# Two mixing layers of a fused float32 model: input columns by pairs of heads, head steps between quarters of the projections, roots of norms on GpSimd

## The chip, the cores and the metric

One program on one core of a Trainium2 chip, one launch. The metric is the device time of the launch in microseconds (us), the median over runs. All data is float32, and the program streams 533.57 MB through the core.

## The reference, cut to what matters

The model is an embedding norm, two layers (a hybrid mixer, then a dense FFN in layer 0 and a mixture of experts in layer 1), then a second block (FFN, gating with dilated attention, cross attention, FFN). The change is in the two hybrid mixers, and in small operations of the dilated attention.

```python
def hybrid_mixer(x, w_in, q_norm_g, kv_norm_g, w_uq, w_ukv, beta_mla, beta_moba, w_o, ...):
    h = x @ w_in                                  # (256, 1024) @ (1024, 2656)
    c_q, c_kv, k_rope, rq, rk, rv, rg, mq, mk, mv = jnp.split(h, splits, axis=-1)
    o_a = rms_norm(mla_attention(c_q, c_kv, k_rope, ...), beta_mla)   # 6 heads, softmax
    o_b = retention(rq, rk, rv, rg, cos_b, sin_b)                     # 5 heads, no softmax, gated
    o_c = rms_norm(moba_attention(mq, mk, mv), beta_moba)             # 5 heads, softmax
    return jnp.concatenate([o_a, o_b, o_c], axis=-1) @ w_o            # (256, 1024) @ (1024, 1024)
```

The MLA heads take queries and keys of 96 columns from two small products (`w_uq`, `w_ukv`) of the normed latents `c_q`, `c_kv`. The other heads have 64 columns. Sequence length is 256: with 128 partitions, every matrix has two row tiles, t = 0 and 1.

## The kernel before, in words

Every weight matrix is cut into chunks of at most 128 x 2048 and streamed by SyncE into a ring of six `raw` buffers. A product in float32 is made of three products in a faster format: ScalarE copies a chunk into `whi` (the high part, L837), VectorE subtracts it and leaves the rest in `wlo` (the low part, L1158), and TensorE runs `mm3` (L350 to L352): whi x high, wlo x high, whi x low part of the activations. `whi` and `wlo` have three slots each (`SPLIT`). The calls `advance(n)` in the streams of ScalarE and VectorE fix where these splits stand in the in-order queue of each engine. The order of all work is written out by hand, engine by engine, with semaphores: `ev0`/`ev1` count evacuated row tiles, `s`, `sf`, `mx`, `p`, `tp`, `pt`, `od`, `o` count the stages of heads, `sd` the square roots, `xh`/`xt` the high and low parts of turned activations.

One mixer runs in four stages, one after the other:

1. `project` (PE): `x @ w_in` in five groups of 512 columns (two chunks each: a group has 4 quarters of 12 matmuls, by half of the depth and row tile) and a last group of 96. ScalarE (L880) and VectorE (L1239) evacuate to `h`. Squares, square roots (L1026, L1027 on ScalarE), scaling and turning of the latents lie beside it, and so does one rotation of all ten retention queries and keys at 128 x 320.
2. The two latent products, `ukv` and `uq`.
3. `heads`: 16 heads, 5 retention, 5 MoBA, 6 MLA, as a software pipeline over steps. A head is turned (q and k, four transposes, L615), copied to `qkt` (ScalarE, L977), scored (L632, L633; retention L629, L630), masked (VectorE, L1417), its maximum taken (L1429, L1430), exponentiated (ScalarE, L981, L983), turned again (L641), copied (L1425), multiplied with v (L659 to L661) and divided (L1443). Everything has two PSUM banks. The retention norm (`retention_sums`, L1374 to L1382, and `retention_norm`, L1390, L1394), and the norms of MoBA and MLA with their square roots on ScalarE (L989, L996, L1048) are placed in it or after it.
4. All of `r` is turned (`transpose_x`, L366), split, and multiplied with `w_o` (two groups of 512 columns, in PSUM banks 4 to 7).

The dilated attention of the second block uses the same `heads` code with 8 heads.

## Time and profile before

| | |
|---|---|
| median of 3 runs | 2351.25 us (2330.93 to 2351.82) |
| span of the profiled execution | 2349.9 us, 1.35 us less than the median |
| mean granted TensorE clock | 0.929 |
| instructions | 27258 |

No time of its own is recorded for the profiled execution besides its span; what lies around it is taken as the 1.35 us between the span and the median. In the rows below, a line of a timeline is: start, duration, engine, source line, operation, output <- inputs, shapes, count, and in brackets the idle time before it with what ended it. A matmul's duration includes its pipeline; the pace of matmuls is read from the distance of their starts. PEclk is the granted clock as a share of full speed: 1.00 is 2.4 GHz, 0.50 is 1.2 GHz.

### The profile page before, as it was taken

To read this page: it belongs to the slowest core of one execution; us is meant where nothing else is said; L and a number is where in the kernel's file an instruction comes from. 1 tells how busy PE (TensorE), PEld (TensorE's weight loads), DVE (VectorE), ACT (ScalarE), POOL (GpSimd) and SP (SyncE) were. 2 spreads that over 40 slices of the span, in tenths; PEclk is the share of its full clock that TensorE was granted. 3 is DMA by queue.
4 is the path that set the end of the run, shared out by engine and by line. 5 is a ranking of instruction groups with operands and counts; after the bars stand their busy time and mean duration, and the time that the engine had idled before them with its cause. 6 is when DMAs were issued, how large, how long until landed. Compare 5 with 4: busy or idle time off the path is not lost.

```text
span 2349.9 us, 27258 instructions
## 1 busy us (share of the span) xinstructions
PE 2177.7 (93%) x9892; PEld 1789.4 (76%) x9892; DVE 1539.9 (66%) x1558; ACT 1260.3 (54%) x1323; POOL 10.8 (0%) x24
## 2 busy tenths in 40 slices
PE   6978998998699999989999999999799888988997
PEld 5856886876578887878787888878588776877886
DVE  5555545644678888878887888888645564544443
ACT  4343343433367677767776677777443445434433
POOL 0000000000000000000000000000000000000000
PEclk9869999956799999999999999999899995999999
DMA  7304554411289999979997998999455350433550
GB/s 296 144 1 152 188 188 146 155 54 54 101 315 362 352 352 352 352 302 348 353 362 307 345 362 341 362 351 373 164 184 191 128 212 1 179 126 118 194 182 35
DMA packets 74407, 533.57 MB, mean 227 GB/s; under 512 B 8432, under 2 KB 8432, under 8 KB 10448
## 3 DMA queue, kind: packets, MB, share of 16 engines
q1 hardware_dynamic: 72000, 519.77, 58.6%
q0 software_dynamic: 2320, 12.56, 1.5%
q8 instruction: 65, 1.06, 0.2%
q14 instruction: 22, 0.18, 0.0%
HBM read 531.25 MB, written 1.05 MB: 227 GB/s over the span
## 4 chain that ended last, share of the span: by engine, by line
PE 89%; DVE 6%; ACT 3%; issue 1%; DMA 1%; POOL 0%; DVEq 0%; ACTq 0%; SPq 0%; POOLq 0%
PE ps L350 26%; PE ps L352 26%; PE ps L351 26%; PE ps L486 1%; PE ps L537 1%; PE ps L515 1%; PE ps L366 1%; PE ps L633 1%; PE ps L615 1%; PE ps L659 1%; PE ps L632 1%; PE ps L458 1%; ACT whi L837 1%; PE ps L641 1%; PE ps L661 1%
## 5 line engine op out<-in xcount | busy, mean ns | idle before, releaser
L1158 DVE TENSOR_TENSOR wlo<-raw,whi 128x2048 fp32r<-128x2048 f32 x500 | 1135.4, 2274 | 440.6 <-ACT whi L837 436.4
L837 ACT ACTIVATE whi<-raw 128x2048 fp32r<-128x2048 f32 x500 | 949.7, 1901 | 342.6 <-PE ps L352 332.2
L350 PE MATMUL ps<-whi,xth 128*128 128x512 f32 (+1 forms) x1872 | 749.3, 400 | 25.4 <-DVE wlo L1158 10.1
L352 PE MATMUL ps<-whi,xtl 128*128 128x512 f32 (+1 forms) x1872 | 731.8, 391 | 0.0
L351 PE MATMUL ps<-wlo,xth 128*128 128x512 f32 (+1 forms) x1872 | 731.0, 390 | 0.0
L350 PEld LDWEIGHTS ps<-whi,xth 128*128 128x128 f32 x1872 | 358.3, 191 | 100.7 <-issue 20.2
L352 PEld LDWEIGHTS ps<-whi,xtl 128*128 128x128 f32 x1872 | 357.8, 191 | 75.4
L351 PEld LDWEIGHTS ps<-wlo,xth 128*128 128x128 f32 x1872 | 359.0, 192 | 70.2 <-issue 1.7
L350 PE MATMUL ps<-whi,hth 128*128 128x512 f32 (+2 forms) x736 | 287.5, 391 | 6.6 <-DVE htl L1260 4.5
L352 PE MATMUL ps<-whi,htl 128*128 128x512 f32 (+2 forms) x736 | 286.6, 389 | 0.0
L351 PE MATMUL ps<-wlo,hth 128*128 128x512 f32 (+2 forms) x736 | 286.0, 389 | 0.0
L350 PEld LDWEIGHTS ps<-whi,hth 128*128 128x128 f32 x736 | 139.2, 189 | 35.0 <-issue 5.4
L352 PEld LDWEIGHTS ps<-whi,htl 128*128 128x128 f32 x736 | 139.1, 189 | 27.9
L351 PEld LDWEIGHTS ps<-wlo,hth 128*128 128x128 f32 x736 | 139.2, 189 | 27.3
L928 ACT ACTIVATE prob<-ps 128x256 f32<-128x256 f32 x112 | 43.0, 384 | 91.7 <-PE ps L352 91.7
L893 ACT ACTIVATE prob<-ps 128x256 f32<-128x256 f32 x66 | 21.7, 381 | 126.0 <-PE ps L352 126.0
L934 ACT ACTIVATE hth<-ps 128x256 fp32r<-128x256 f32 x112 | 43.1, 384 | 82.7 <-PE ps L515 82.7
L897 ACT ACTIVATE hth<-ps 128x512 fp32r<-128x512 f32 x33 | 19.8, 599 | 104.3 <-PE ps L458 104.3
L1255 DVE TENSOR_TENSOR probt<-prob,ps 128x256 f32<-128x256 f32 x66 | 24.9, 418 | 66.6 <-ACT prob L893 66.6
L1417 DVE SCALAR_TENSOR_TENSOR prob<-ps,cst 128x384 f32<-128x384 f32 x30 | 16.7, 557 | 67.8 <-PE ps L633 67.8
L1260 DVE TENSOR_TENSOR htl<-ps,hth 128x512 fp32r<-128x512 f32 x33 | 22.8, 691 | 55.3 <-ACT hth L897 55.3
L366 PE MATMUL ps<-cst,r 128*128 128x128 f32 x112 | 23.8, 400 | 34.3 <-DVE r L1234 22.1
(276 smaller groups left out, 1510.5 us busy)
## 6 DMA issues: line engine op xcount, KB each, us to landing
raw<-in_stream SPq DMA_DIRECT2D x493, 1024.0 KB, 4.8
bc<-in_rows POOLq DMA_DIRECT2D x5, 1024.0 KB, 5.1
cst<-in_consts POOLq DMA_DIRECT2D x1, 2180.0 KB, 12.6
raw<-in_stream SPq DMA_DIRECT2D x4, 384.0 KB, 3.1
raw<-in_stream SPq DMA_DIRECT2D x2, 576.0 KB, 3.6
r<-in_x POOLq DMA_DIRECT2D x2, 512.0 KB, 4.6
bc<-in_rows POOLq DMA_DIRECT2D x2, 512.0 KB, 4.4
bc<-in_mem POOLq DMA_DIRECT2D x1, 1024.0 KB, 5.1
```

The source lines that it names most:

```text
L350: pe.matmul(o, ah, bh, start=start, stop=False, skip_group_check=True)
L351: pe.matmul(o, ah, bl, start=False, stop=False, skip_group_check=True)
L352: return pe.matmul(o, al, bh, start=False, stop=stop, skip_group_check=True)
L366: m = pe.transpose(ps[banks[k // 2]][:, (k % 2) * S + t * P:(k % 2) * S + (t + 1) * P], src[:, t, k * P:(k + 1) * P], ident)
L458: m = pe.transpose(ps[2][:, k * S + t * P:k * S + (t + 1) * P], hs[:, t, k * P:(k + 1) * P], ident)
L486: m = pe.matmul(ps[bank][:, k * P:(k + 1) * P], x[:, t, (4 * g + k) * P:(4 * g + k + 1) * P], onehot[:, e, t, :], start=(t == 0), stop=(t ...
L515: m = pe.transpose(ps[1][:, k * P:(k + 1) * P], hs[:, 0, k * P:(k + 1) * P], ident)
L837: act.activation(whi[:, c.split, 0:c.width], raw[:, c.raw, 0:c.width], ACT.Copy).then_inc(hi_done, 1)
L928: act.activation(sg[:, 0, :], ps[0][:, 0:FU], ACT.Silu).then_inc(sem("e_sg"), 1)
L934: act.activation(hth[:, 0:2, 0:P], ps[1][:, 0:2 * P].rearrange("p (k s) -> p k s", k=2), ACT.Copy).then_inc(sem("e_hh"), 1)
L1158: dve.tensor_tensor(wlo[:, c.split, 0:c.width], raw[:, c.raw, 0:c.width], f32(whi[:, c.split, 0:c.width]), ALU.subtract).then_inc(lo_done, 1)
L1255: m = dve.tensor_tensor(hs[:, t, :], sg[:, t, :], ps[t][:, FU:2 * FU], ALU.mult)
```

## The change

- **Layout and widths.** The input columns are reordered on the host: latents and one gate (480), then five groups with q, k, v of a *pair* of heads and the gate of one retention head (448, 448, 448, 448, 384). All six groups come in two chunks (12 in place of 11), and the latent weights come after the fourth chunk. Each row tile of a group has a PSUM bank of 4 to 6.
- **Pairs.** q and k of a pair are turned together (four transposes for two heads); the second head of a pair is scored from partitions 64 to 127 of `qkt`. The order of heads is retention 0, 1, MLA 0 to 5, retention 2, 3, 4, MoBA 0 to 4 (`WORK`).
- **Placement.** Step i of the pipeline does turn(i), outputs(i-3) or, for retention, outputs(i-2), turn_p(i-2), scores(i-1). Steps 0 to 13 stand behind quarters of groups 2 to 5, steps 14 and 15 behind the last quarter, 16 to 18 between quarters of the first half (by depth) of the output product. The turning of `r` and the output product are in two halves: depth 0 to 511 (MLA and two retention heads) first. The stages of a head have one PSUM bank each (scores bank 0, turned probabilities bank 1, turned q and k bank 7), only the outputs have two.
- **Masks.** Mask and maximum are one `tensor_tensor_reduce` per row tile (`masked`), the division is one `tensor_tensor` for both (`normed`); this holds for the dilated heads too.
- **Roots.** Reciprocal square roots of the latent, retention, MLA and MoBA norms are computed by GpSimd (`inverse_root`: multiply-add, then power -0.5). The retention gate uses Tanh in place of Silu, with one more VectorE operation (`retention_gates`).
- **Rotation** of retention queries and keys is done by pairs, for both row tiles in one operation (`rotate_pair`), at the start and in steps 2 and 6.

```diff
+PAIRS = ((("ret", 0), ("ret", 1)), (("ret", 2), ("ret", 3)), (("ret", 4), ("moba", 0)),
+         (("moba", 1), ("moba", 2)), (("moba", 3), ("moba", 4)))
+PAIR_OF = {head: (p, s) for p, pair in enumerate(PAIRS) for s, head in enumerate(pair)}
+
+
+WORK = (list(PAIRS[0]) + [("mla", n) for n in range(MLA_H)] + list(PAIRS[1]) + list(PAIRS[2]) + list(PAIRS[3])
+        + list(PAIRS[4]))
...
+IN_GROUPS = 6
+IN_WIDTHS = [C_PAIR, W_PAIR, W_PAIR, W_PAIR, W_PAIR, W_PAIR - HD]
+STEPS_BY_GROUP = {2: {3: [0], 4: [1]}, 3: {1: [2], 2: [3], 3: [4], 4: [5]}, 4: {1: [6], 2: [7], 3: [8], 4: [9]},
+                  5: {1: [10], 2: [11], 3: [12], 4: [13]}}
+ROTATE_AT = {2: 1, 6: 2}
+GATES_AT, MLA_SQUARES_AT, RET_SUMS_AT, SCALE_AT = 10, 12, 13, 14
+B_TQ, B_S, B_TP, B_O = 7, 0, 1, 2
...
+    _in = [KD // 2 * _w for _w in IN_WIDTHS for _ in range(2)]
+    STREAM += [(f"in{_l}", _in[0:4]), (f"uq{_l}", [2 * 576]), (f"ukv{_l}", [768]), (f"inb{_l}", _in[4:]),
+               (f"o{_l}", PROJ * 2)]
...
+            def inverse_root(ready, dst, means, eps_value):
+
+                pool.wait_ge(*ready)
+                for a, b, src, scale in means:
+                    m = pool.tensor_scalar(var[:, a:b], src, scale, eps_value, ALU.mult, ALU.add)
+                link(m)
+                pool.tensor_tensor(dst, var[:, means[0][0]:means[-1][1]], half[:, 0:means[-1][1] - means[0][0]],
+                                   ALU.pow).then_inc(sem("rs"), 1)
...
                 rows(2 + 4 * l, 2, ("emb" if l == 0 else "ln2_0", "x"), T)
+                inverse_root(at(f"lat{l}", "sq", 1), rstd[:, :], ((0, 2, ss[:, 0:2], 1.0 / 256), (2, 4, ss[:, 2:4], 1.0 / 128)), RMS_EPS)
+
+                inverse_root((sem(f"ret{l}_var"), 1), gs[:, 3, 0:10], ((4, 14, gs[:, 1, 0:10], 4.0 / HD),), 4.0 * RMS_EPS)
+                inverse_root(at(f"mla{l}", "sq", 1), rstd[:, 0:2], ((0, 2, ss[:, 0:2], 1.0 / 384),), RMS_EPS)
+                inverse_root(at(f"moba{l}", "sq", 1), rstd[:, 2:4], ((2, 4, ss[:, 2:4], 1.0 / 320),), RMS_EPS)
...
+                def step(i):
+
+                    if i < len(WORK):
                         turn_qk(i)
-                    if 0 <= i - 3 < len(work) and not soft[i - 3]:
+                    if 0 <= i - 3 < len(WORK) and SOFT[i - 3]:
                         outputs(i - 3)
-                    if i >= 4 and soft[i - 4]:
-                        outputs(i - 4)
-                    if 3 <= i < len(work) + 3:
-                        turn_p(i - 3)
-                    if 1 <= i < len(work) + 1:
+                    if 0 <= i - 2 < len(WORK) and not SOFT[i - 2]:
+                        outputs(i - 2)
+                    if 0 <= i - 2 < len(WORK) and SOFT[i - 2]:
+                        turn_p(i - 2)
+                    if 0 <= i - 1 < len(WORK):
                         scores(i - 1)
...
+                for j, t in ((0, 0), (0, 1), (1, 0), (1, 1)):
+                    in_part(0, j, t)
+                for j, t in ((0, 0), (0, 1), (1, 0)):
+                    in_part(1, j, t)
+                transpose_x(f"lat{l}", h, kn=3, banks=(0, 1))
+                in_part(1, 1, 1)
+                pe.wait_ge(*at(f"lat{l}", "xt", 1))
+                latent(f"uq{l}", 288, (0, 2), lambda t, part: UQ_BANKS[2 * t + part], free_uq)
+                pe.wait_ge(*at(f"lat{l}", "xt", 2))
+                latent(f"ukv{l}", 384, (2, 3), lambda t, part: 2 * t + part, lambda t, part: None)
+                for g in range(2, IN_GROUPS):
+                    for n, (j, t) in enumerate(((0, 0), (0, 1), (1, 0), (1, 1))):
+                        in_part(g, j, t)
+                        for i in STEPS_BY_GROUP[g].get(n + 1, ()):
+                            step(i)
+                step(14)
+                step(15)
+                turn_mix(0, (5, 7))
+                o_part(0, 0, 0)
+                step(16)
+                o_part(0, 0, 1)
+                step(17)
+                o_part(0, 1, 0, range(0, 2))
+                step(18)
+                o_part(0, 1, 0, range(2, 4))
+                o_part(0, 1, 1)
+                turn_mix(1, (0, 1))
+                for n in range(2):
+                    for t in range(T):
+                        o_part(1, n, t)
 
             pe.wait_ge(sem("ident_in"), 16)
...
+            def softmax(stage, n, count):
+
+                act.wait_ge(*at(stage, "mx", count))
+                act.activation(prob[:, n % 2, 0:P], prob[:, n % 2, 0:P], ACT.Exp, bias=nmax[:, n, 0:1], scale=-1.0,
+                               accum_out=rsum[:, n, 0:1])
+                act.activation(prob[:, n % 2, P:3 * P], prob[:, n % 2, P:3 * P], ACT.Exp, bias=nmax[:, n, 1:2], scale=-1.0,
+                               accum_out=rsum[:, n, 1:2]).then_inc(sem("p"), 1)
...
+                def step(i):
+
+                    g = 2 + i // 4
+                    if g < IN_GROUPS and i % 4 < 2:
+                        evac_in(g, i % 4)
+                    if i < len(WORK) and (i == 0 or UNIT_OF[i - 1] != UNIT_OF[i]):
+                        u = UNIT_OF[i]
+                        d = QD if UNITS[u][0] == "mla" else P
+                        act.wait_ge(*at(hd, "tq", u + 1))
+                        act.activation(qkt[0:d, u % 2, :], ps[B_TQ][0:d, :], ACT.Copy).then_inc(sem("qk"), 1)
+                    if i % 2 == 0:
+                        advance(in_chunk(l, 7 + i // 2) if i <= 8 else AT[f"o{l}"] + min((i - 10) // 2, 2))
+                    if 0 <= i - 1 < len(WORK) and SOFT[i - 1]:
+                        softmax(hd, i - 1, soft_before(i))
+                    if i == GATES_AT:
...
+                    if i == MLA_SQUARES_AT:
+                        act.wait_ge(*at(hd, "o", WORK.index(("mla", MLA_H - 1)) + 1))
+                        act.wait_ge(sem(f"gated{l}"), 1)
+                        squares(f"mla{l}", [(r[:, t, 0:384], h[:, t, 0:384], ss[:, t:t + 1]) for t in range(T)])
+
...
+            def masked(n, bank, mask, scale):
+
+
+                for t, a, b in ((0, 0, P), (1, P, 3 * P)):
+                    m = dve.tensor_tensor_reduce(out=prob[:, n % 2, a:b], in0=ps[bank][:, a:b], in1=mask[:, a:b], scale=-scale,
+                                                 scalar=-NEG, op0=ALU.add, op1=ALU.min, accum_out=nmax[:, n, t:t + 1])
...
+            def normed(stage, n, bank, col, count):
+
+                dve.wait_ge(*at(stage, "od", n + 1))
+                dve.wait_ge(*at(stage, "ri", count))
+                dve.tensor_tensor(r[:, :, col:col + HD], ps[bank][:, 0:2 * HD].rearrange("p (t d) -> p t d", t=T),
+                                  rinv[:, n, :].unsqueeze(2).to_broadcast([P, T, HD]), ALU.mult).then_inc(sem("o"), 1)
...
+                def step(i):
+
+                    if 0 <= i - 3 < len(WORK) and SOFT[i - 3]:
+                        dve.reciprocal(rinv[:, i - 3, :], rsum[:, i - 3, :]).then_inc(sem("ri"), 1)
+                        take_outputs(i - 3)
+                    if 0 <= i - 2 < len(WORK) and not SOFT[i - 2]:
+                        take_outputs(i - 2)
+                    if 0 <= i - 2 < len(WORK) and SOFT[i - 2]:
+                        n = i - 2
+                        dve.wait_ge(*at(hd, "tp", soft_before(n + 1)))
+                        dve.tensor_copy(probt[:, n % 2, 0:3 * P], ps[B_TP][:, 0:3 * P]).then_inc(sem("pt"), 1)
+                    if 0 <= i - 1 < len(WORK):
+                        weigh(i - 1)
+                    if i % 2 == 0:
+                        advance(in_chunk(l, 7 + i // 2) if i <= 8 else AT[f"o{l}"] + min((i - 10) // 2, 2))
+                    if i == 17:
+                        advance(AT[f"o{l}"] + 3)
+                    if i in ROTATE_AT:
+                        rotate_pair(ROTATE_AT[i])
+                    if i == GATES_AT:
+                        retention_gates()
+                    if i == RET_SUMS_AT:
+                        retention_sums()
+                    if i == SCALE_AT:
+                        retention_norm()
+                        scale(f"mla{l}", 0, 0, 384)
+
+                advance(in_chunk(l, 3))
+                dve.wait_ge(*at(st, "ev0", 1))
...
+                    link(dve.tensor_copy(kc[:, t, :, NOPE:QD],
+                                         h[:, t, C_ROPE:C_RG].unsqueeze(1).to_broadcast([P, MLA_H, ROPE])))
+                dve.sem_inc(sem(f"kv{l}"), 1)
+                rotate_queries()
+                advance(in_chunk(l, 6))
...
+                split_mix(0, (5, 7))
+                for i in range(16, 19):
+                    step(i)
+                scale(f"moba{l}", 2, O_MOBA, D)
+                split_mix(1, (0, 1))
 ```

On TensorE, a step of the MLA heads in layer 0 (L615, L791: turn q and k; L659 to L661, L834 to L836: outputs; L641, L819: turn probabilities; L632/L633, L811/L812: scores). Before:

```order
L615 MATMUL ps<-cst,qc 96x128 [waits qk]
L615 MATMUL ps<-cst,qc 96x128
L615 MATMUL ps<-cst,kc 96x128 x2
L659 MATMUL ps<-h,probt 128x64 [waits o,pt]
L660 MATMUL ps<-h,probt 128x64
L661 MATMUL ps<-h,probt 128x64
L641 MATMUL ps<-cst,prob 128x128 [waits p]
L641 MATMUL ps<-cst,prob 128x128 x2
L632 MATMUL ps<-qkt 128x128 [waits sf,qk]
L633 MATMUL ps<-qkt 128x256
```

In the changed kernel a step, and the beginning of the quarter of twelve matmuls that follows it (L420 to L422 are `mm3`):

```order
L791 MATMUL ps<-cst,qc 96x128 [waits rope0,qk]
L791 MATMUL ps<-cst,qc 96x128
L791 MATMUL ps<-cst,kc 96x128 x2
L834 MATMUL ps<-vc,probt 128x64 [waits o,pt]
L835 MATMUL ps<-vc,probt 128x64
L836 MATMUL ps<-vc,probt 128x64
L819 MATMUL ps<-cst,prob 128x128 [waits pt,p]
L819 MATMUL ps<-cst,prob 128x128 x2
L811 MATMUL ps<-qkt 128x128 [waits mx,qk]
L812 MATMUL ps<-qkt 128x256
L420 MATMUL ps<-whi,xth 128x448 [waits lo_done]
L421 MATMUL ps<-wlo,xth 128x448
```

Before, the next step follows at once; now a quarter of the input product stands between two steps, and the scores wait for the maximum of the head before.

On VectorE, the retention norm's sums in layer 0 (L1374 to L1382, L1681 to L1689). Before, in step 10 of `heads`, with nine steps to come:

```order
L1443 TENSOR_SCALAR r<-ps,rinv 128x64
L1374 TENSOR_REDUCE gs<-r 128x10 [waits o]
L1375 TENSOR_SCALAR gs<-gs 128x10 [waits dve_chain]
L1378 TENSOR_TENSOR r<-r,gs 128x320 [waits dve_chain]
L1378 TENSOR_TENSOR r<-r,gs 128x320
L1381 TENSOR_TENSOR h<-r 128x2x320 [waits dve_chain]
L1382 TENSOR_REDUCE gs<-h 128x10 [waits dve_chain]
L1417 SCALAR_TENSOR_TENSOR prob<-ps,cst 128x384 [waits s]
```

In the changed kernel they stand in step 13; what follows them in step 14, up to the split of an output chunk (L1403) and the norm (L1707, L1710), is:

```order
L1689 TENSOR_REDUCE gs<-h 128x10 [waits dve_chain]
L1752 RECIPROCAL rinv<-rsum 128x2
L1624 TENSOR_TENSOR r<-ps,rinv 128x2x64 [waits ri,od]
L1759 COPY probt<-ps 128x384 [waits tp]
L1616 ISA prob,nmax<-ps,cst 128x128 [waits s]
L1616 ISA nmax 128x1
L1616 ISA prob,nmax<-ps,cst 128x256
L1616 ISA nmax 128x1
L1403 TENSOR_TENSOR wlo<-raw,whi 128x2048 [waits hi_done]
L1707 TENSOR_TENSOR r<-r,gs 128x320 [waits rs]
L1707 TENSOR_TENSOR r<-r,gs 128x320
L1710 TENSOR_TENSOR r<-r,h 128x2x320 [waits dve_chain]
```

The sums, a chunk's split and the norm now stand in three successive steps, with head work that TensorE waits for behind each of them.

On ScalarE, the end of the heads in layer 0: squares of MLA, square root and split of all of `r`. Before:

```order
L1046 ACTIVATE prob,ss<-r 128x384 [waits o]
L1046 ACTIVATE prob,ss<-r 128x384
L1048 ACT_TABLE_LOAD
L1048 ACTIVATE sd<-ss,eps 128x2 [waits act_chain]
L855 ACTIVATE xth<-ps,cols 128x256 [waits tr]
```

In the changed kernel, the squares of MoBA (the root is on GpSimd) and the split of the second half:

```order
L1216 ACTIVATE h,ss<-r 128x320 [waits o]
L1216 ACTIVATE h,ss<-r 128x320
L1225 ACTIVATE xth<-ps,cols 128x256 [waits tr]
L1225 ACTIVATE xth<-ps,cols 128x256
L1225 ACTIVATE xth<-ps,cols 128x256 [waits tr]
```

The table load and the root are gone from ScalarE's queue, and between the squares and the split there is now GpSimd, VectorE's scaling and TensorE's turning.

## Rows read from the trace of the kernel before

**Rows 1.** The page: busy time of the engines, and the chain by engine.

```profile
PE 2177.7 (93%) x9892; PEld 1789.4 (76%) x9892; DVE 1539.9 (66%) x1558; ACT 1260.3 (54%) x1323; POOL 10.8 (0%) x24
PE 89%; DVE 6%; ACT 3%; issue 1%; DMA 1%; POOL 0%; DVEq 0%; ACTq 0%; SPq 0%; POOLq 0%
```

**Rows 2.** Busy time by stage; columns in the first line, the first is the stretch.

```profile
core 0: us, PE busy (x) PEld busy (x) DVE busy (x) ACT busy (x) POOL busy (x), PEclk, DMA share, GB/s
23.45:195.84 172.39, 156.52 (x699) 128.50 (x699) 90.45 (x188) 67.80 (x124) 0.00 (x0) 0.81 0.32 123
86.81:92.32 5.51, 5.51 (x38) 5.27 (x37) 2.97 (x3) 4.64 (x3) 0.00 (x0) 1.00 0.34 144
92.32:171.95 79.63, 63.76 (x273) 50.68 (x274) 40.84 (x134) 31.54 (x87) 0.00 (x0) 0.62 0.07 27
409.85:587.78 177.93, 163.93 (x699) 135.44 (x699) 90.20 (x191) 70.34 (x128) 0.00 (x0) 0.75 0.25 90
479.80:565.89 86.09, 72.09 (x274) 57.38 (x274) 40.31 (x134) 31.32 (x87) 0.00 (x0) 0.52 0.06 22
1938.90:1981.40 42.50, 38.27 (x136) 27.71 (x136) 16.89 (x58) 17.32 (x48) 0.00 (x0) 0.50 0.00 1
```

**Rows 3.** TensorE's timeline: 512-column matmuls at full clock.

```profile
193.80 0.39 PE L350 MATMUL ps<-whi,xth 128*128 128x512 f32 x1
...
195.61 0.39 PE L352 MATMUL ps<-whi,xtl 128*128 128x512 f32 x1
```

**Rows 4.** TensorE's timeline: one MLA step at full clock, to the next step's start.

```profile
142.64 0.43 PE L659 MATMUL ps<-h,probt 128*128 128x64 f32 x2 [0.73 <-DVE probt L1425]
...
144.57 0.38 PE L615 MATMUL ps<-cst,kc 128*96 128x128 f32 x2
145.69 0.43 PE L659 MATMUL ps<-vc,probt 128*128 128x64 f32 x2 [0.74 <-DVE probt L1425]
```

**Rows 5.** Groups by line and form, 23.45 to 195.84: count, busy us, mean ns.

```profile
L1158 DVE TENSOR_TENSOR wlo<-raw,whi 128x2048 fp32r<-128x2048 f32 x15 | 34.3, 2291 | 32.4 <-ACT whi L837 31.1 <-issue 1.3
...
L1417 DVE SCALAR_TENSOR_TENSOR prob<-ps,cst 128x384 f32<-128x384 f32 x11 | 6.1, 557 | 19.7 <-PE ps L633 19.7
...
L1425 DVE COPY probt<-ps 128x384 f32<-128x384 f32 x11 | 5.9, 540 | 1.2 <-PE ps L641 1.2
...
L983 ACT ACTIVATE prob<-prob,nmax 128x256 f32<-128x256 f32 x11 | 5.4, 493 | 0.0
...
L1430 DVE TENSOR_REDUCE nmax<-prob 128x1 f32<-128x256 f32 x11 | 4.5, 409 | 0.0
...
L1429 DVE TENSOR_REDUCE nmax<-prob 128x1 f32<-128x128 f32 x11 | 3.0, 277 | 0.1
```

**Rows 6.** VectorE's timeline: the retention sums, first and last instruction.

```profile
134.88 0.81 DVE L1374 TENSOR_REDUCE gs<-r 128x10 f32<-128x640 f32 x1
...
137.72 0.82 DVE L1382 TENSOR_REDUCE gs<-h 128x10 f32<-128x640 f32 x1
```

**Rows 7.** Timeline from the turning of `r` to the output product, layer 0.

```profile
167.62 3.68 PE L366 MATMUL ps<-cst,r 128*128 128x128 f32 x16 [3.99 <-DVE r L1515]
170.06 2.30 ACT L855 ACTIVATE xth<-ps,cols 128x256 fp32r<-128x256 f32 x6 [3.15 <-PE ps L366]
...
171.95 0.77 PE L350 MATMUL ps<-whi,xth 128*128 128x512 f32 x1 [0.65 <-DVE xtl L1178]
```

**Rows 8.** Windows with the granted clock (columns as in rows 2).

```profile
94.80:128.00 33.20, 33.13 (x119) 26.16 (x120) 12.12 (x45) 9.82 (x23) 0.00 (x0) 0.50 0.12 49
140.00:154.00 14.00, 10.02 (x75) 8.28 (x74) 8.38 (x31) 9.08 (x28) 0.00 (x0) 1.00 0.00 0
466.00:470.00 4.00, 4.00 (x38) 4.00 (x36) 2.05 (x2) 1.41 (x2) 0.00 (x0) 0.98 0.51 203
470.00:474.00 4.00, 4.00 (x18) 4.00 (x19) 0.26 (x1) 0.87 (x1) 0.00 (x0) 0.50 0.71 258
```

**Rows 9.** GpSimd's groups, the whole run.

```profile
L336 POOL DMA_DIRECT2D kc<-in_spatial x1 | 0.9, 905 | 0.0
...
L311 POOL MEMSET eps<- 128x1 f32 x1 | 0.1, 98 | 0.3 <-POOLq L1833 0.3
```

717 lines of the change are left out of this document (422 added, 295 removed).

## The prediction, made before the changed kernel was run

> **What bounds the kernel now.** I read the page first: TensorE is busy 93% of the span and makes up 89% of the chain that ended last, far ahead of VectorE at 6% [rows 1]. So only two things shorten the run: less TensorE work, or the same work at a better pace. Next the windows by stage [rows 2]: a mixer, from the first input matmul to the last output matmul, takes 172.39 us in layer 0 and 177.93 in layer 1, together 350.3. Of these, the heads with the turning of `r` take 79.63 and 86.09. In both, TensorE is busy for only 63.76 and 72.09, and the granted clock is 0.62 and 0.52: this stage pays for waits and for the slow clock. Last the timelines, for the price of one piece.
>
> At full clock 512-column matmuls start 0.226 apart (8 steps from 193.80 to 195.61, [rows 3]). Narrow ones do not follow their columns all the way: the 96-column group issues 38 in 4.00 us, 0.105 each [rows 8]. An MLA step takes 3.05 us, of which 0.74 is waiting, so 2.31 are work [rows 4]. A MoBA step saves half of its turning with pairs (0.28), a retention step also the turning of probabilities (0.33; both estimates from the same step): 2.03 and 1.70.
>
> **TensorE's work after the change, at full clock, per mixer.** By columns from 0.226 per 512: 480, 448 and 384 columns cost 0.212, 0.199 and 0.172. The input product has 48 matmuls of each group: 48 x (0.212 + 4 x 0.199 + 0.172) = 56.6. Before it is 48 x (5 x 0.226 + 0.105) = 59.3, so 2.7 us of narrow matmuls go. Latent products 5.2 (their 36 matmuls in the 5.51 of [rows 2]), turning of latents 0.8. Heads: 6 x 2.31 + 5 x 2.03 + 5 x 1.70 = 32.5. Output product 96 x 0.226 = 21.7. Turning of `r` 1.8.
>
> **What hides what.** A quarter of a 448-column group is 12 x 0.199 = 2.4 us and now stands between two steps. Between the scores of a head and its turn_p TensorE has this quarter, a turning and the outputs of an older head: 2.4 + 0.45 + 0.7 = 3.5 us. The other engines need in that time the mask with maximum and two exponentials. The exponentials I take as 1.35 (0.493 for the wide one, [rows 5], a little less for the narrow one, two readouts). `tensor_tensor_reduce` does not occur in the trace. Below, it is bounded by the mask alone, 0.56, above by twice mask and two maxima, 2 x (0.56 + 0.41 + 0.28) = 2.5 [rows 5]. I take 1.0, nearest to the 1.25 of the three operations that it replaces. With 0.2 for semaphores the chain is 2.6, so it fits, unless a split (2.29 for a full chunk, [rows 5]) or a rotation stands ahead in VectorE's queue. Going through steps 0 to 13 by these prices, VectorE is late four times: 0.4 at the start (evacuation of k and v and rotation of queries before the split of the seventh chunk), 1.9 at step 4 (a split and a rotation of six operations stand before the first softmax head's mask), 0.2 and 0.6 later. That is 3.1 us of stall. For the latent chain, three quarters (7.2 us) hide evacuation, squares, root and scaling (about 3.8), so it costs nothing; GpSimd has 3.4 us of slack there.
>
> So from the first input matmul to the end of step 13: 56.6 + 0.8 + 5.2 + head work of steps 0 to 13, which is 32.5 less 7.3 for what stands later (five outputs, four turn_p, three scores, a turning) = 25.2, + stalls 3.1 = 90.9. The first 13 matmuls of layer 0 and the first 5 of layer 1 still run at half clock, as before: + 2.6 and + 1.0.
>
> **The tail.** Here no quarters are left, and VectorE sets the pace. From the end of step 13 on TensorE: mask of head 12 1.35 (it starts behind the split of a chunk); sums of the retention norm 3.6 (134.88 to 138.54, [rows 6]); step 14: division, copy, mask 2.05 (0.5 + 0.54 + 1.0), split 2.3, norm and scaling 2.5 (about two thirds of the sums: two instructions of 320, one of 640, two of 384 columns); step 15: 2.05. Sum 13.9. Before, these sums stood beside eight more heads. Then the exponentials of head 14 (1.35), which stand in ScalarE's queue before the split of the first half of `r`, and 1.9 from its start to the first output matmul (170.06 to 171.95, [rows 7]): 17.2. Then two quarters of 2.7 with step 16 of 1.8 between, 7.2, and 3.1 more for the part of it at half clock, since TensorE has stood idle several times before. Then high and low part of the last output chunk in a row, 1.95 + 2.3; behind it on VectorE stand the last head's division 0.5, squares 0.95, GpSimd's root 0.6, scaling 0.7; TensorE's three remaining quarters (2.7 each, and steps 17 and 18) lie beside this. Then turning and split 2.9, and the second half of the output product, 48 x 0.226 = 10.9. Together 17.2 + 10.3 + 4.3 + 2.75 + 2.9 + 10.9 = 48.4.
>
> GpSimd's two instructions are bounded by the smallest and largest of its rows, 2 x 0.1 and 2 x 0.9 [rows 9]; I take 0.6. Only the MoBA root is exposed. The retention root has 4.3 us of cover (step 14 up to the split); this cover is VectorE's own queue.
>
> The Trainium skill (GPSIMD Engine Reference, Instruction dispatch) says that the first call of a freshly loaded kernel pays about 6 us that no instruction shows. No run here shows it yet. By it the first latent root would outlast its 3.4 us of slack by about 3 us, once, and the sum would be 3 us higher.
>
> **Sum.** Layer 0: 90.9 + 2.6 + 48.4 = 141.9; layer 1: 90.9 + 1.0 + 48.4 = 140.3; together 282.2 against 350.3, a gain of 68.1. The table loads for square roots that stood on the path are in the stages that are replaced whole. The dilated heads run at 0.50 and TensorE is busy 38.27 of 42.50 [rows 2], so a shorter softmax chain gives nothing; the longer mask instruction now stands before the copy that the outputs wait for, about 0.4 late in eight steps less what is covered: + 1.5. Everything else is unchanged. 2349.9 - 68.1 + 1.5 = 2283.3, and with the 1.35 around the span 2284.7; I give 2285.
>
> **Rivals.**
> A. *Chains bind every step.* The mask instruction costs its upper bound 2.5, and copies of `qkt`, evacuations and high parts (1.9) stand before the exponentials on ScalarE. Then the 3.5 us between scores and turn_p do not suffice. Price: 1.5 more less 0.9 slack, some ten steps, 6 us; 1.5 in each of three tail steps, 4.5; one GpSimd root at its upper bound, 1.2; ScalarE's order 0.5 in ten steps, 5: 16.7 per mixer, 33 in all, 2318. For it: single PSUM banks make each step wait for the one before. Against: VectorE was busy only 90 of 172 us in a mixer and has little more to do now.
> B. *The clock stays at half in the interleaved stretch* (slower). From group 2 to the middle of the output product there are 36.8 + 10.9 of dense matmuls and 32.5 of head work. At half clock these double, + 80, less stalls and waits that it swallows (about 16): 64 per mixer, 128 in all, 2413. It decides from about half of the stretch at half clock on, where the gain of 68 is gone. For it: 33 us of head work without a gap ran at 0.50 [rows 8], and in layer 1 the clock fell at 470 in the middle of 96-column matmuls, with TensorE busy without a gap [rows 8]. Against: before those narrow ones, 512-column matmuls held 1.00, and head work with 4 us of 14 idle held 1.00 from 140 to 154. The Trainium skill (TensorE: Matmul & The Clock Gate, HAM oscillation) blames idle gaps alone; by that rule the stretch stays at full clock, but the trace does not agree at 470, so B stays open.
> C. *Better cover in the tail.* If VectorE works through sums, mask and split faster than I priced (mask at 0.56) and the clock does not fall there: 4 + 3.1 + 3.1 of stalls, 10 per mixer, 2265.
>
> **How the numbers follow.** Forecast 58%, A 23%, B 8% (a third of it only part of the stretch, near 2350), C 11%. About what can be told from no change here is 1%, 24 us. Faster by over 1% needs less than 2327.7: forecast, C and nearly all of A give 0.88; B in part and A at its worst 0.06 within 1%; B in full 0.06 slower. The range takes in C and A with its bounds: 2255 to 2330, which leaves out B.
>
> **What would show it.** Right: from group 2 on TensorE starts a quarter within about 0.1 of the end of a step, at clock 1.00; MLA steps at a period near 4.7 us; VectorE without idle from the sums to the split of `r`; TensorE idle about 11 us around steps 14 and 15 (17.2 less the 6 or so of work in it), and a clock of 0.50 after it. A mixer takes 140 to 142 us. Wrong: turn_p waiting for the exponentials in each step (A), PEclk of 0.50 in the windows of groups 3 to 5 (B), a GpSimd instruction of several us before the latents' scaling, or a `tensor_tensor_reduce` far from 0.5 us per instruction.

## The result, and the profile after

The changed kernel takes 2277.78 us (median of 4 runs, 2271.92 to 2278.76) against 2341.09 for the kernel before beside it: a ratio of 0.970, 95% interval 0.966 to 0.974. Timed again later (a_again2) it took 2266.12 (2264.79 to 2279.18), ratio 0.971 (0.967 to 0.974). The forecast was 2285 us. The kernel before spreads wider than the changed one, from 2328.49 to 2351.82 us in its four runs here, and its trace (span 2349.9) is of one of the longest, while the trace of the changed kernel (span 2270.1) is of the shortest of its four. So the gain is 63 us by the medians here, 78 by those of a_again2 and its neighbours (2344.02 before), and 79.8 between the two traces.

The page after, with the lines that answer to [rows 1]:

```profile
PE 2117.5 (93%) x9852; PEld 1752.4 (77%) x9852; DVE 1517.7 (67%) x1556; ACT 1249.0 (55%) x1313; POOL 24.2 (1%) x43
PE 90%; DVE 6%; ACT 2%; issue 1%; DMA 1%; POOL 0%; DVEq 0%; SPq 0%; ACTq 0%; POOLq 0%
```

The shares say almost nothing: TensorE was the bound and still is. What shows the change is the busy time by stage, to be read beside [rows 2]. First the whole mixer of layer 0, from the first input matmul to the end of the last output matmul, then layer 1's, then the dilated heads:

```profile
21.73:159.05 137.32, 128.70 (x679) 112.14 (x679) 82.21 (x187) 61.03 (x118) 6.60 (x9) 0.95 0.43 155
...
373.32:508.21 134.89, 126.81 (x679) 110.78 (x679) 81.66 (x190) 63.25 (x122) 6.60 (x9) 0.94 0.37 131
...
1855.44:1896.89 41.45, 36.84 (x134) 26.54 (x135) 11.99 (x58) 17.21 (x48) 0.00 (x0) 0.51 0.00 1
```

The mixers went from 172.39 + 177.93 = 350.3 us to 272.2: 78.1 of the 79.8 us by which the span fell (2349.9 to 2270.1). TensorE's busy time in them fell by 65 (320.5 to 255.5) and its idle time by 13 (29.9 to 16.7), and the granted clock rose from 0.81 and 0.75 to 0.95 and 0.94. With two levels only, twice the missing share is the time at half clock: an estimate from these rows is 154 us before and 30 after. So the larger part of the gain is the same work at the faster clock. The remaining 1.7 us is a sum of small differences of both signs, of which one is chance: TensorE waits once or twice in a run, 5 to 6 us each, for weights among the experts' chunks (once in the changed kernel, `PE ps L420 <- DVE wlo L1403: 5.8, 1, 5.8` between 700 and 1500 us; 10.9 in two for e2_two_part_mask below). What lies outside the mixers, which no edit below but those of the mask touches, takes 1987.5 (e3_roots_scalar) to 2004.2 us (e6_apart_filled) in the traces; these waits are a part of that spread. It moves whole runs by more than some edits below are worth. So I compare the mixers in the traces (from the start of the first input matmul to 0.23 us behind the start of the last output matmul) and the times beside them.

Where the half clock went is shown by windows along layers 0 and 1:

```profile
30.00:110.00 80.00, 80.00 (x467) 73.30 (x466) 50.12 (x127) 42.00 (x76) 1.42 (x3) 1.00 0.48 173
110.00:120.00 10.00, 6.71 (x41) 5.27 (x40) 9.44 (x22) 7.08 (x20) 2.23 (x3) 0.96 0.32 106
120.00:130.00 10.00, 6.65 (x20) 4.82 (x21) 6.60 (x18) 2.45 (x9) 2.07 (x2) 0.50 0.28 107
130.00:140.00 10.00, 10.00 (x48) 8.06 (x47) 2.51 (x10) 2.91 (x5) 0.00 (x0) 0.86 0.00 0
...
380.00:460.00 80.00, 80.00 (x468) 73.34 (x467) 50.09 (x127) 42.05 (x76) 1.42 (x3) 1.00 0.43 154
```

In these 80 us (quarters and latent products, and from 57.95 on steps between the quarters) TensorE has no idle time and clock 1.00. Then the quarters are used up: 6.7 of 10 us busy, VectorE 9.44 of 10, and the clock falls. TensorE's timeline of one MLA step with its quarter, to the next step:

```profile
76.89 0.38 PE L791 MATMUL ps<-cst,qc 128*96 128x128 f32 x2
...
77.94 0.50 PE L819 MATMUL ps<-cst,prob 128*128 128x128 f32 x3
...
78.50 0.60 PE L812 MATMUL ps<-qkt 96*128 96x256 f32 x2
78.75 0.56 PE L420 MATMUL ps<-whi,xth 128*128 128x448 f32 x1
...
81.38 0.38 PE L791 MATMUL ps<-cst,qc 128*96 128x128 f32 x2
```

The quarter starts at 78.75, straight behind the scores, and the next step comes 4.49 us after this one, without a bracket of idle time. Before, a step alone took 3.05 with 0.74 of waiting [rows 4], at full clock, which it had for a small part of the stage only.

VectorE's timeline in the tail, from the mask of head 12 to the scaling:

```profile
113.30 0.28 DVE L1616 CUSTOM_DVE_ANT_0 prob<-ps,cst 128x128 f32<-128x128 f32 x1
113.50 0.08 DVE L1616 DVE_READ_ACCUMULATOR2_ANT nmax<- 128x1 f32 x1
113.50 0.42 DVE L1616 CUSTOM_DVE_ANT_0 prob<-ps,cst 128x256 f32<-128x256 f32 x1
113.85 0.08 DVE L1616 DVE_READ_ACCUMULATOR2_ANT nmax<- 128x1 f32 x1
113.85 0.81 DVE L1681 TENSOR_REDUCE gs<-r 128x10 f32<-128x640 f32 x1
...
118.91 2.29 DVE L1403 TENSOR_TENSOR wlo<-raw,whi 128x2048 fp32r<-128x2048 f32 x1
121.12 0.89 DVE L1707 TENSOR_TENSOR r<-r,gs 128x320 f32<-128x320 f32 x2
...
122.78 0.74 DVE L1715 TENSOR_SCALAR r<-r,rstd 128x384 f32<-128x384 f32 x2
```

No line carries an idle bracket, and none does until the mask of head 14 ends at 125.01: up to there this queue sets the pace. Then ScalarE's exponential of head 14 and its split of `r` stand on the path:

```profile
125.05 0.40 ACT L1182 ACTIVATE prob<-prob,nmax 128x128 f32<-128x128 f32 x1 [5.03 <-DVE nmax L1616]
...
125.94 1.54 ACT L1225 ACTIVATE xth<-ps,cols 128x256 fp32r<-128x256 f32 x4
```

TensorE's three longest waits (outputs of head 12, turning of `r`, first output matmul; the last is for both engines) are:

```profile
118.50 0.43 PE L834 MATMUL ps<-h,probt 128*128 128x64 f32 x2 [2.10 <-DVE probt L1759]
...
123.25 1.97 PE L860 MATMUL ps<-cst,r 128*128 128x128 f32 x8 [0.70 <-DVE r L1715]
127.80 0.77 PE L420 MATMUL ps<-whi,xth 128*128 128x512 f32 x1 [2.58 <-DVE xtl L1723]
```

### The profile page after: what moved, and what is told of

Read it like the earlier page. It is cut to its first block, busy times and chain, and to the rows that moved or that the text cites. A ratio compares the mean times of both kernels' runs of the same rounds, so it can differ in the third digit from the quotient of the medians.

```text
span 2270.1 us, 27254 instructions
## 1 busy us (share of the span) xinstructions
PE 2117.5 (93%) x9852; PEld 1752.4 (77%) x9852; DVE 1517.7 (67%) x1556; ACT 1249.0 (55%) x1313; POOL 24.2 (1%) x43
## 4 chain that ended last, share of the span: by engine, by line
PE 90%; DVE 6%; ACT 2%; issue 1%; DMA 1%; POOL 0%; DVEq 0%; SPq 0%; ACTq 0%; POOLq 0%
PE ps L420 27%; PE ps L422 27%; PE ps L421 26%; PE ps L554 1%; PE ps L605 1%; PE ps L583 1%; DVE wlo L1403 1%; PE ps L436 1%; ACT whi L1045 1%; PE ps L526 1%; DVE r L1459 0%; DVE resid L1450 0%; PE ps L791 0%; DMA raw<-in_stream 0%; DVE xtl L1417 0%
## 5 line engine op out<-in xcount | busy, mean ns | idle before, releaser
L1403 DVE TENSOR_TENSOR wlo<-raw,whi 128x2048 fp32r<-128x2048 f32 (+4 forms) x502 | 1135.4, 2265 | 401.9 <-ACT whi L1045 397.3
L1045 ACT ACTIVATE whi<-raw 128x2048 fp32r<-128x2048 f32 (+4 forms) x502 | 950.1, 1894 | 284.2 <-PE ps L422 281.2
L420 PE MATMUL ps<-whi,xth 128*128 128x512 f32 (+3 forms) x1872 | 754.4, 403 | 26.8 <-DVE wlo L1403 10.2
L422 PE MATMUL ps<-whi,xtl 128*128 128x512 f32 (+3 forms) x1872 | 732.0, 391 | 0.0
L421 PE MATMUL ps<-wlo,xth 128*128 128x512 f32 (+3 forms) x1872 | 731.3, 391 | 0.0
L420 PEld LDWEIGHTS ps<-whi,xth 128*128 128x128 f32 x1872 | 359.2, 192 | 101.9 <-issue 21.5
L421 PEld LDWEIGHTS ps<-wlo,xth 128*128 128x128 f32 x1872 | 359.8, 192 | 67.2 <-issue 1.7
L420 PE MATMUL ps<-whi,hth 128*128 128x512 f32 (+2 forms) x736 | 286.5, 389 | 6.6 <-DVE htl L1505 4.5
L421 PE MATMUL ps<-wlo,hth 128*128 128x512 f32 (+2 forms) x736 | 285.0, 387 | 0.0
L420 PEld LDWEIGHTS ps<-whi,hth 128*128 128x128 f32 x736 | 138.5, 188 | 35.0 <-issue 5.4
L421 PEld LDWEIGHTS ps<-wlo,hth 128*128 128x128 f32 x736 | 138.5, 188 | 27.3
L1136 ACT ACTIVATE prob<-ps 128x256 f32<-128x256 f32 x112 | 43.0, 384 | 91.9 <-PE ps L422 91.9
L1105 ACT ACTIVATE hth<-ps 128x512 fp32r<-128x512 f32 x33 | 19.7, 598 | 104.4 <-PE ps L526 104.4
L436 PE MATMUL ps<-cst,resid 128*128 128x128 f32 x64 | 15.7, 427 | 38.2 <-DVE resid L1450 38.2
L1546 DVE TENSOR_TENSOR htl<-ps,hth 128x256 fp32r<-128x256 f32 x112 | 46.8, 418 | 0.0
```

The costliest lines, as they stand in the source:

```text
L420: pe.matmul(o, ah, bh, start=start, stop=False, skip_group_check=True)
L421: pe.matmul(o, ah, bl, start=False, stop=False, skip_group_check=True)
L422: return pe.matmul(o, al, bh, start=False, stop=stop, skip_group_check=True)
L436: m = pe.transpose(ps[banks[k // 2]][:, (k % 2) * S + t * P:(k % 2) * S + (t + 1) * P], src[:, t, k * P:(k + 1) * P], ident)
L1045: act.activation(whi[:, c.split, 0:c.width], raw[:, c.raw, 0:c.width], ACT.Copy).then_inc(hi_done, 1)
L1136: act.activation(sg[:, 0, :], ps[0][:, 0:FU], ACT.Silu).then_inc(sem("e_sg"), 1)
```

## The experiments

Mixer lengths are those of layers 0 and 1 in the profiled run. The changed kernel has 137.3 and 134.9 (136.0 and 134.7 in a_again2).

**a_again2: the changed kernel unchanged.**

> The changed kernel as it is, timed beside the kernels of this group: 2272 to 2280 us, mixers of 137.3 and 134.9 us in the trace.

Measured: 2266.12 us, below the range I gave, with mixers 1.3 and 0.2 us shorter than in the first trace. Differences of some 1.5 us in a mixer and of 10 us between medians therefore say nothing by themselves. Each mixer length here is from one trace.

**e1_apart: the input side of the placement undone.** The evacuations and splits of groups 2 to 5 move ahead of the steps on ScalarE and VectorE too.

```
-  in_part(g, j, t)
-  for i in STEPS_BY_GROUP[g].get(n + 1, ()):
-      step(i)
-step(14)
+  in_part(g, j, t)
+for i in range(15):
+    step(i)
```

> The changed kernel with one thing undone: steps 0 to 13 of the heads all follow the last quarter of the input product (pairs, masks in one instruction and roots on GpSimd stay). Theory (the placement carries the gain, because the steps' TensorE work of 25 us then runs at clock 1.00 and their chains lie beside the quarters): set apart, the same steps run at clock about 0.5 and wait for VectorE and ScalarE, 50 to 58 us instead of 25, so each mixer grows by 25 to 33 us, and the time is 2328 to 2345 us. Rival (the gain comes from less work: pairs of heads, masks, roots): the mixers grow by no more than 8 us each, under 2295 us.

Measured: 2310.72 us (2304.36 to 2318.82), ratio to before 0.988 (0.982 to 0.994); mixers 155.9 and 151.6. Between theory and rival: steps 0 to 13 take 43.0 us (89.80 to 132.84) and not 50 to 58. The windows show why:

```profile
89.80:114.00 24.20, 17.56 (x123) 14.51 (x121) 13.54 (x57) 11.81 (x34) 0.00 (x0) 1.00 0.00 1
114.00:134.90 20.90, 18.43 (x68) 14.77 (x69) 11.77 (x28) 8.79 (x19) 0.00 (x0) 0.52 0.23 82
```

The clock stayed at 1.00 for 24 us of steps with TensorE idle a quarter of the time, and fell afterwards. In that first part the MLA steps come 2.96 us apart (turnings at 105.11 and 108.07), against 2.31 of work: the chain through mask and exponential sets them. So the 18.6 and 16.7 us that the mixers grew come from both, chains in the open and, later, half clock.

**e2_two_part_mask: the mask in two kinds of instruction.**

```
-m = dve.tensor_tensor_reduce(out=prob[..], in0=ps[bank][..], in1=mask[..], scale=-scale,
-                             scalar=-NEG, op0=ALU.add, op1=ALU.min, accum_out=nmax[..])
+link(dve.scalar_tensor_tensor(out=prob[..], in0=ps[bank][..], scalar=-scale, in1=mask, op0=ALU.mult, op1=ALU.add))
+m = dve.tensor_reduce(nmax[..], prob[..], AX, ALU.min)      # twice
```

> The changed kernel, its masks in two kinds of instruction again (scale and mask over 384 columns, then two minima), in both mixers and in the dilated heads. A mask then takes about 1.35 us instead of the 0.63 that the changed kernel's trace shows. Theory (VectorE is on the path only in the tail): in steps 0 to 13 it is hidden; steps 14 to 16 hold two masks on the path, +1.5 us a layer, and the last two dilated heads +1 each: 5 us more in all, 2281 to 2286 us. Rival (VectorE paces every step): 11 soft heads at 0.72 us in both layers, 16 us more, 2294 us.

Measured: 2280.86 us, ratio 0.974 (0.969 to 0.978); mixers 138.8 and 138.5, together 5.1 more. The median is at the theory's size. The traces show 9.0 us: beside the 5.1, 3.9 in the dilated heads (45.34 us from 1864.79 to 1910.13, where the changed kernel has 41.45). The rival's 16 us would be in the mixers and are not. The longer mask takes 1.20 us (113.56 to 114.76), and even so TensorE waits only once, 0.19 us, between 30 and 112 us.

**e5_apart_mask: both together.** Head steps apart, and the longer mask.

> e1_apart (steps 0 to 13 behind the whole input product) and e2_two_part_mask (the mask in two kinds of instruction) in one kernel. Between the quarters the longer mask cost 5.1 us over both mixers (138.8 and 138.5 against 137.3 and 134.9). Theory (quarters cover the chains, and without them the chain of a step, scores to mask to exponential to turning, sets the pace): with the steps apart the 0.72 us of 11 soft heads come back in full and TensorE idles more, so its clock falls earlier; each mixer is 8 to 15 us longer than in e1_apart (155.9 and 151.6), time 2327 to 2341 us. Rival (the mask costs the same wherever the steps stand): 2 to 3 us a mixer, about 2316 us.

Measured: 2331.17 us, ratio 0.995 (0.992 to 0.998); mixers 164.8 and 161.9 (21.21 to 186.04 and 399.95 to 561.82), 8.9 and 10.2 more than e1_apart. The same edit costs 19.1 us with the steps apart and 5.1 beside the quarters. The theory holds, at the lower end of its range.

**e7_output_apart: the output side of the placement undone.**

```
+for i in range(16, 19):
+    step(i)
 turn_mix(0, (5, 7))
 o_part(0, 0, 0)
-step(16)
 o_part(0, 0, 1)
-step(17)
-o_part(0, 1, 0, range(0, 2))
-step(18)
-o_part(0, 1, 0, range(2, 4))
+o_part(0, 1, 0)
```

> The changed kernel with the output side of the placement undone: steps 16 to 18 stand ahead of the turning of the mixture and the output product, steps 0 to 13 stay between the input quarters. Theory (the last two heads' chains lie beside the first output quarters): mask, exponential, turning and copy of heads 14 and 15 are then waited for, the first output matmul comes 7 to 9 us later, of which the 3.6 us of work of steps 16 to 18 and the waits before the second turning come back: 2 to 5 us a mixer, 2277 to 2287 us against the 2266 to 2278 us of the changed kernel. Rival (VectorE's queue sets the time of the output product anyway, so the heads' place there does not matter): mixers within 1 us of 137.3 and 134.9.

Measured: 2280.80 us, ratio 0.971 (0.969 to 0.973); mixers 142.7 and 140.9, 5.4 and 6.0 more. The first output matmul starts at 136.00 instead of 127.80. The theory's direction holds, its price of 2 to 5 us a mixer was too low, and the rival is out. The whole time is 3 us above the changed kernel's first median and 15 above its second, so it tells nothing finer.

**e8_all_apart: both sides apart and the longer mask.**

> Both sides of the placement and the one-instruction mask undone together (e5_apart_mask and e7_output_apart in one kernel). What then is left of the change are the pairs of heads with their layout of the input columns, the roots on GpSimd, and the joint division. Theory (placement and mask are nearly the whole gain): mixers of 166 to 171 us, 2340 to 2350 us, the kernel before within 1%. Rival (pairs and the rest of the work saved are worth more than that): mixers no longer than e5_apart_mask's 163.5 and 159.8 us, 27 us below the kernel before.

Measured: 2341.83 us, ratio 0.998 (0.995 to 1.001); mixers 170.8 and 168.3. The theory holds. (The mixers of e5_apart_mask in the expectation were read too short; they are the 164.8 and 161.9 above, and the rival is out by either.) With the mixers of before (350.3) this makes a ledger of the 78.1 us, in this order: everything else (pairs with their layout, roots, joint division, rotation by pairs, the output product in halves) 11.2 (to 339.1); output side of the placement 12.4 (to 326.7); short mask 19.1 (to 307.6); input side 35.4 (to 272.2). The order matters: the mask is worth 5.1 and the output side 11.3 when taken away alone from the changed kernel. The 11.2 are the difference of two traces; the medians beside each other differ by 5.0 us, with an interval of the ratio that takes in 1, and how the 11.2 divide was not tried.

**e3_roots_scalar: square roots on ScalarE, reciprocals on VectorE.**

```
-inverse_root(at(f"mla{l}", "sq", 1), rstd[:, 0:2], ...)     # GpSimd, and three more
+act.activation(sd[:, n:n + 2], ss[:, n:n + 2], ACT.Sqrt, bias=eps[:, 1:2], scale=1.0 / width)
+link(dve.reciprocal(rstd[:, n:n + T], sd[:, n:n + T]))
```

> The changed kernel with the roots of the mixers' norms on ScalarE again (square root with its table load, then a reciprocal on VectorE). Theory (GpSimd saves table loads only where ScalarE is awaited): the retention and MLA roots hide behind VectorE's split, the latents' behind the product, and only the last root, +1.3 us of table load and +0.2 of reciprocal less 0.9 of GpSimd, shows: 1 to 3 us more in all, 2279 to 2281 us. Rival (every table load is on the path): four a layer at 1.3 us, 10 us more, 2288 us.

Measured: 2275.79 us (2266.05 to 2277.99), ratio 0.972 (0.968 to 0.976); mixers 139.1 and 137.5, 1.8 and 2.6 more. ScalarE's timeline with three of the table loads:

```profile
121.44 1.28 ACT L1255 ACT_TABLE_LOAD   x1
...
123.24 1.28 ACT L1177 ACT_TABLE_LOAD   x1
127.45 0.40 ACT L1177 ACTIVATE prob<-prob,nmax 128x128 f32<-128x128 f32 x1 [2.93 <-DVE nmax L1622]
...
146.00 1.28 ACT L1209 ACT_TABLE_LOAD   x1
```

The load at 123.24 costs nothing: it lies in a wait for VectorE that lasts to 127.45. The one at 121.44 is seen: VectorE's norm waits for this root, and TensorE's wait ahead of the first turning grew from 0.70 to 1.71 us. So is the last, at 146.00, ahead of the MoBA root. By the mixers 4.4 us in all, between theory (1 to 3) and rival (10), and not far above the 1.5 that two traces of one kernel differ by; by the whole time no difference that can be told.

**e4_keep_busy: matmuls that nobody reads in the three waits of the tail.**

```
+keep_busy(8)     # matmul(ps[4], hth[:, 2, 0:P], hth[:, 0:2, :]), 512 columns
 step(15)
+keep_busy(3)
 turn_mix(0, (5, 7))
+keep_busy(10)
 o_part(0, 0, 0)
```

> The changed kernel, with 8, 3 and 10 matmuls of 512 columns that nobody reads placed in TensorE's three waits between the input and the output product (before step 15, before the turning of the mixture, behind it). Theory (what follows the waits runs at clock 0.50 because TensorE stood idle in them): the clock stays at 1.00, the turning takes 1.1 us instead of 1.97 and the first output quarter 2.8 instead of 5.1, 3 to 4 us less a layer, 2270 to 2272 us. Rival 1 (the clock falls for the steps' small matmuls and not for the idle time): clock still 0.5 there, the extra matmuls take 0.43 us each and push the work behind them back, 5 us or more slower. Rival 2 (VectorE sets the whole tail): within 1 us of the changed kernel.

Measured: 2273.91 us, ratio 0.971 (0.967 to 0.975); mixers 135.6 and 133.3, 1.7 and 1.6 less, half of what I expected (against a_again2 only 0.4 and 1.4 less, which is within what two traces differ by). In layer 0 the clock was 1.00 from 110 to 120 and 0.83 from 120 to 130; the turning still took 1.97 us at 121.99, and the first output quarter ran at full clock. In layer 1 the clock was 1.00 from 460 to 500 and the turning took 1.09 us at 471.05. So there the theory's account of the clock holds whole, and the mixer is hardly shorter all the same: behind the ten fillers TensorE still waits 1.14 us for VectorE's split.

**e6_apart_filled: e1_apart with matmuls that nobody reads in the steps.**

```
 def turn_p(i):
+    if i < 12:
+        keep_busy(3)
```

> e1_apart with three matmuls of 512 columns that nobody reads ahead of the turning of the probabilities in steps 2 to 13 (0.68 us at full clock, where e1_apart's MLA steps let TensorE wait 0.70 us). In e1_apart the clock was 1.00 until 114 us and 0.50 from there to the first output matmuls. Theory (idle waits in the steps let the clock fall): it stays at 1.00 through step 13, steps 8 to 13 take their 16 us at 3 us each or less instead of 21, and a mixer is 4 to 8 us shorter than in e1_apart, 2295 to 2303 us. Rival (the steps' small matmuls let it fall, however closely they follow each other): clock 0.50 from about 114 us all the same, and the extra matmuls at 0.43 us each make it longer than e1_apart.

Measured: 2311.51 us, ratio 0.988 (0.983 to 0.992); mixers 153.3 and 154.0 (e1_apart 155.9 and 151.6): no gain.

```profile
110.00:120.00 10.00, 9.15 (x58) 7.19 (x57) 5.58 (x22) 5.58 (x13) 0.00 (x0) 0.97 0.01 2
120.00:130.00 10.00, 9.81 (x32) 6.87 (x31) 6.64 (x13) 4.41 (x10) 0.00 (x0) 0.50 0.29 105
```

In layer 0 the clock fell some 5 us later than in e1_apart, at the retention steps, where no fillers stand ahead and each matmul is short. TensorE was busy 9.15 and 9.81 of 10 us around the fall, and its longest wait there is 0.71 us. In layer 1 the clock fell at the first steps already (0.66 from 460 to 470, TensorE busy 9.17 of the 10 us before), which in e1_apart it did not. Long idle waits do not explain this.

**b1_tail_cut: less of VectorE's queue in the tail.** ScalarE's split of `r` also moves, ahead of the exponential of head 14.

```
-  advance(.. AT[f"o{l}"] + min((i - 10) // 2, 2))   # at i == 14; now at 16
-if i == RET_SUMS_AT: retention_sums()
+if i == RET_SUMS_AT - 2: retention_sums(0, 4)       # heads 0 to 3
+if i == RET_SUMS_AT: retention_sums(4, 5)
-  retention_norm()
+  retention_norm(0, 2)                              # (2, 5) behind split_mix(0)
```

> The changed kernel with VectorE's work between step 13 and the first output quarter cut: sums of retention heads 0 to 3 at step 11, where VectorE waits 2.5 us for TensorE (head 4 stays at step 13), the low part of the third output chunk behind the first split of the mixture (2.3 us), the gated norm of heads 2 to 4 there too (1.0 us), and ScalarE splits the mixture before the exponential of head 14 (0.9 us). Theory (VectorE sets the pace of that stretch, 113.9 to 127.8 us): the first output matmul comes 4 to 6 us earlier in each layer, mixers of 132 and 130 us, 2266 to 2270 us. Rival (GpSimd's root of 1.96 us and the heads' own chain take VectorE's place): 1 to 2 us a layer, 2274 to 2276 us.

Measured: 2264.92 us (2255.08 to 2272.61), ratio 0.968 (0.964 to 0.972); mixers 131.8 and 132.2. The first output matmul comes 101.4 us after the first input matmul, not 106.1. The theory holds; what ScalarE's part in it is worth (0.9 us by the expectation) was not tried alone.

**b2_tail_cut_filled: b1_tail_cut with fillers (4, 2 and 8).**

> b1_tail_cut with 4, 2 and 8 matmuls of 512 columns that nobody reads at the three places of e4_keep_busy. With them e4_keep_busy's clock was 0.83 in its slice from 120 to 130 us instead of 0.50, and its mixers 1.7 and 1.6 us shorter (135.6 and 133.3). Theory (a part of the time at clock 0.50 comes from idle waits): the first output quarter, 4.3 us long in b1_tail_cut, takes about 3 us, mixers of 130 to 131 us, 2262 to 2264 us. Rival (in b1_tail_cut the waits are so short already that the extra matmuls only stand in the way): the mixers get 1 to 2 us longer.

Measured: 2263.68 us (2259.93 to 2265.87), ratio 0.967 (0.963 to 0.970); mixers 129.0 and 129.7, 2.8 and 2.5 less than b1_tail_cut, and clock 1.00 from 110 to 150 in layer 0 (in layer 1 it fell for a short time later, 0.83 from 480 to 490). The theory holds, slightly better than forecast. The median of the whole time differs from b1_tail_cut's by 1.2 us, less than its spread.

**b3_turn_early: b1_tail_cut taken further.** Head 4's sums, root and norm go behind `split_mix(0)`, a GpSimd root of their own for them, and:

```
-step(15)
 turn_mix(0, (5, 7))
+step(15)
```

> b1_tail_cut taken further: the sums, root and norm of retention head 4 go behind the first split of the mixture, GpSimd's first retention root covers heads 0 to 3 alone, the norm of heads 0 and 1 and the scaling of the MLA part stand at the end of VectorE's step 13, and TensorE turns the first half of the mixture ahead of step 15 instead of behind it. Theory (in b1_tail_cut TensorE and VectorE waited for ScalarE's exponential at 115 to 116 us and for GpSimd's root of 1.96 us, and the turning came behind them): the turning comes 2 to 3 us earlier and lies beside the exponential of head 13, the first output matmul 2 to 4 us earlier than in b1_tail_cut, mixers of 129 and 129 us, 2259 to 2263 us. Rival (the heads' own chain of steps 14 and 15 sets the time of the first output quarter, wherever the turning stands): no change against b1_tail_cut's mixers of 131.8 and 132.2 us.

Measured: 2253.22 us (2244.21 to 2258.93), ratio to before 0.963 (0.959 to 0.966); mixers 126.9 and 127.1. Better than both kernels, and better than I expected by 2 us a mixer. TensorE turns at 115.83 straight behind step 14, at full clock, and the first output matmul follows at 119.38:

```profile
115.83 1.09 PE L868 MATMUL ps<-cst,r 128*128 128x128 f32 x8
...
119.38 0.47 PE L428 MATMUL ps<-whi,xth 128*128 128x512 f32 x1 [0.33 <-DVE xtl L1734]
```

```profile
110.00:120.00 10.00, 8.86 (x56) 6.93 (x56) 7.92 (x23) 6.25 (x23) 1.94 (x3) 1.00 0.29 106
120.00:130.00 10.00, 10.00 (x58) 8.25 (x57) 9.18 (x29) 5.71 (x10) 0.89 (x2) 1.00 0.19 48
```

In layer 0 the clock never falls, with no filler. In layer 1 it holds through the same place (1.00 from 450 to 470) and falls for a short time behind it (0.86 from 470 to 480, TensorE busy 8.00 of 10 us). What I had not counted is that shortening the queue gives most of the half-clock time back as well.

## Why the prediction was right

It named 2285 us; 2277.78 was measured, and rivals A (2318) and B (2413) did not come. The mechanism is the one it named, steps hidden between quarters at full clock and a tail that VectorE paces. That the first median lies within 7 us is in part luck: the sum was 10 us too long in the mixers, a_again2 (2266.12) lies at rival C's number (2265), and two medians of the one kernel differ by 12 us. Point by point:

- **Sum of the mixers.** Predicted 141.9 + 140.3 = 282.2, measured 272.2: a gain of 78.1 and not 68.1.
- **Input product and steps 0 to 13.** Predicted 93.5 and 91.9 with the half-clock start; measured 91.3 (21.73 to 113.01) and 89.6 (373.32 to 462.95). *The step that failed is the term of 3.1 us of stalls*: between 30 and 110 us TensorE does not wait once. The price of the mask is not what was wrong with it. `tensor_tensor_reduce` took 0.63 with both readouts (113.30 to 113.93) for my 1.0, but with 1.20 in its place (e2_two_part_mask) TensorE still waits only 0.19 us. The two exponentials took 0.99 (113.97 to 114.96) for my 1.35. Which other price in the walk through VectorE's queue was too long stays open. Pace of 448 columns: 0.203 (three matmuls from 62.46 to 63.07) for my 0.199, and 0.207 where no step stands between (33 matmuls from 50.72 to 57.54); here the other terms were low by about 1. MLA steps came 4.49 us apart for my 4.7.
- **Rival A.** Refuted by the same rows. Its order of queues is real, though: with the steps apart the chain sets 2.96 us a step (e1_apart), and the longer mask costs nearly four times as much (19.1 us for 5.1, e5_apart_mask). The quarters are what hides it.
- **Rival B.** Refuted: the granted clock was 1.00 through both stretches of 80 us. The Trainium skill (TensorE: Matmul & The Clock Gate, HAM oscillation) has idle gaps as the cause of a fall; this stretch without a gap agrees. e6_apart_filled hardly does: there it fell with TensorE busy 9.15 of 10 us and no wait over 0.71 us.
- **Rival C.** Half of it came. Masks were faster (0.63) and the stalls were gone, but the clock did fall in the tail (0.50 from 120 to 130). Of its 10 us a mixer 4.6 and 5.4 were measured.
- **Tail.** Predicted 48.4, measured 46.0 (113.01 to 159.05). By terms: VectorE's stretch to the mask of head 14, 12.0 for 13.9 (three short masks); exponential and split 2.8 for 3.3; two quarters with step 16, 9.9 for 10.3; high and low part 4.4 for 4.3; division to scaling 3.1 for 2.75; turning and split 2.8 for 2.9; second half 11.0 for 10.9. That VectorE paces it up to the mask of head 14 is shown by its queue without a gap; taking work from it (b1_tail_cut, b3_turn_early) shortened the tail, though both also move work of ScalarE, and b3_turn_early TensorE's turning. TensorE's idle time there was 6.6 us (busy 8.26 of the 14.90 from 112.90 to 127.80), where I had said about 11.
- **Tail, layer 1.** 45.3 for 48.4: the same terms, the clock falling earlier (0.86 in the slice 460 to 470) and coming back earlier.
- **GpSimd root.** Predicted 0.6 for the MoBA root, measured 0.96 (143.81 to 144.77). No instruction or gap of several us: the latent root runs from 37.14 to 38.70, 0.09 us behind ScalarE's last squares (end 37.05), and TensorE does not wait. The Trainium skill (GPSIMD Engine Reference, Instruction dispatch) has 6 us for a first call; no run here shows it. That the root saves its table load was right and small (e3_roots_scalar).
- **Dilated heads.** Predicted + 1.5; measured 41.45 to the last outputs, where before has 41.76 (1938.94 to 1980.70): - 0.3. The step that failed here is "a shorter softmax chain gives nothing": with the longer mask in the changed kernel this stretch takes 45.34 (e2_two_part_mask), so the short mask is worth 3.9 us there, and without it the stretch is longer than before.
- **Where the gain came from.** The forecast did not divide it. In the order of the ledger above, the placement brought 47.8 of 78.1 us.
